# First attention rewritten: q and k stacked in high and low parts, P scaled while it is flipped, V stationary, output projection begun early

## The reference, cut to what matters

```
def _fox_attention(x, w_in, b_f, w_out):          # 16 heads of 64
    proj = x @ w_in
    q, k, v = heads of proj[..., :d], [d:2d], [2d:3d]
    c = cumsum(log_sigmoid(proj[..., 3*d:] + b_f))
    logits = q @ k.T * 64**-0.5 + c[q] - c[k]     # causal: k <= q
    p = softmax(logits)
    return merge(p @ v) @ w_out
```

## Time and profile before

| | us |
|---|---|
| median of 3 runs (2490.05 to 2502.78) | 2502.63 |
| the profiled execution | 2500.41 |
| its span, first to last instruction | 2498.2 |
| busy in the span: TensorE, VectorE, ScalarE, GpSimd | 2328.3, 1084.2, 969.5, 827.3 |
| busy from 0 to 340 us, fp32r projection matmuls with 512 columns, three groups | 161.2 |
| the same, plain fp32 value matmuls PS<-aV,aPT, 320 records | 47.7 |

### The profile page before, as it was taken

The page is one execution under the profiler, slowest core; times in us unless marked ns, Lnnn a source line. Parts: engine busy times, 40 slices in busy tenths (PEclk is TensorE's granted clock), DMA queues, the critical chain, the costliest instruction groups (busy, mean ns, idle before and its releaser), DMA issues.

```text
span 2498.2 us, 28179 instructions
## 1 busy us (share of the span) xinstructions
PE 2328.3 (93%) x11008; PEld 1848.6 (74%) x11008; DVE 1084.2 (43%) x1702; ACT 969.5 (39%) x1929; POOL 827.3 (33%) x616
## 2 busy tenths in 40 slices
PE   8999999999989989899999968997899997999997
PEld 6777678888877766678888857664488886888886
DVE  3333355544344566555553342555555233333322
ACT  4333344443235455354443244443244333333221
POOL 1111064433444333444333442002432335322232
PEclk9999899999989998899999969997899997999998
DMA  4011012222312110122222201010012221222221
GB/s 181 34 51 51 34 63 99 92 101 95 105 53 68 51 51 35 51 73 96 101 99 93 103 11 68 34 34 17 1 43 77 101 101 51 102 97 89 97 98 58
DMA packets 26773, 178.88 MB, mean 72 GB/s; under 512 B 2961, under 2 KB 3089, under 8 KB 8849
## 3 DMA queue, kind: packets, MB, share of 16 engines
q1 hardware_dynamic: 26640, 177.08, 20.2%
HBM read 174.97 MB, written 2.10 MB: 71 GB/s over the span
## 4 chain that ended last, share of the span: by engine, by line
PE 88%; DVE 4%; ACT 4%; POOL 2%; issue 2%; DMA 0%; POOLq 0%; ACTq 0%; SPq 0%; DVEq 0%
PE PS L1150 85%; PE PS L1239 1%; POOL XL L2186 1%; PE PS L1330 1%; DVE cCVT L2070 0%; PE PS L1276 0%; POOL A_p L2206 0%; ACT bP L1576 0%; POOL A_c L2206 0%; ACT HI L1418 0%; POOL A_a L2208 0%; DVE bST L1940 0%; DVE YH L1806 0%; PE PS L1256 0%; POOL A_a L2206 0%
## 5 line engine op out<-in xcount | busy, mean ns | idle before, releaser
L2186 POOL TENSOR_TENSOR LO<-RAW,HI 128x512 fp32r<-128x512 f32 (+1 forms) x334 | 483.0, 1463 | 946.4 <-ACT HI L1418 946.4
L1150 PE MATMUL PS<-XH,HI 128*128 128x512 f32 (+1 forms) x1584 | 651.7, 411 | 37.9 <-POOL XL L2186 20.5
L1150 PE MATMUL PS<-XL,HI 128*128 128x512 f32 (+1 forms) x1584 | 625.9, 395 | 0.0
L1150 PE MATMUL PS<-XH,LO 128*128 128x512 f32 (+1 forms) x1584 | 625.9, 395 | 0.0
L1735 DVE TENSOR_TENSOR LO<-RAW,HI 128x512 fp32r<-128x512 f32 (+1 forms) x334 | 359.2, 1080 | 332.4 <-ACT HI L1418 332.1
L1418 ACT ACTIVATE HI<-RAW 128x512 fp32r<-128x512 f32 (+3 forms) x668 | 365.4, 607 | 178.5 <-PE PS L1150 171.7
L1150 PEld LDWEIGHTS PS<-XH,HI 128*128 128x128 f32 (+1 forms) x1584 | 303.1, 191 | 124.4 <-issue 56.0
L1150 PEld LDWEIGHTS PS<-XH,LO 128*128 128x128 f32 (+1 forms) x1584 | 301.5, 190 | 66.1 <-issue 1.4
L1150 PEld LDWEIGHTS PS<-XL,HI 128*128 128x128 f32 (+1 forms) x1584 | 303.1, 191 | 53.5 <-issue 1.1
L1150 PE MATMUL PS<-HH,HI 128*128 128x512 f32 x528 | 205.4, 389 | 0.0
L1150 PE MATMUL PS<-HL,HI 128*128 128x512 f32 x528 | 205.4, 389 | 0.0
(11 more groups left out here) (368 smaller groups left out, 3193.7 us busy)
## 6 DMA issues: line engine op xcount, KB each, us to landing
RAW<-wall SPq DMA_DIRECT2D x138, 1024.0 KB, 4.8
RAW<-wall SPq DMA_DIRECT2D x24, 896.0 KB, 4.6
RAW<-wall SPq DMA_DIRECT2D x5, 512.0 KB, 3.5
XF<-xT SPq DMA_DIRECT2D x4, 512.0 KB, 5.5
outT<-XR SPq DMA_DIRECT2D x8, 256.0 KB, 2.0
FP<-cfp SPq DMA_DIRECT2D x1, 1024.0 KB, 6.8
MKF<-cmask SPq DMA_DIRECT2D x1, 704.0 KB, 11.1
RAW<-wall SPq DMA_DIRECT2D x1, 640.0 KB, 3.9
```

The lines of the kernel that those rows point to most:

```text
L1150: return e.matmul(out, a, b, start=start, stop=stop)
L2186: return e.tensor_tensor(out, x, h.bitcast(F32), ALU.subtract)
```

## The change

- **q and k.** A q tile is evacuated (`qeq`) into four half-height copies by ScalarE (each head's high part on both halves of the 128 rows) and two low parts by VectorE; a k tile (`qek`) into two high parts by ScalarE and two low parts on the other half by VectorE. The other half beside q's low part is filled with zeros once (`zero`). A score block is then two fp32r matmuls over 128 rows and the mask. Everything is double buffered by head pair.
- **P.** The logits and the exponentials share one of three buffers aP. A new step `dg` (VectorE) makes the reciprocal of the row sum and multiplies the identity with it; the flip is a plain fp32 matmul of the P block with this diagonal. A new step `ft` cuts the flipped block into a high part (ScalarE) and a low part (VectorE).
- **Values.** The four steps of a head are now its key blocks. V's high or low part (two heads side by side, 128 columns) is stationary, P moves with 512 to 128 columns, three fp32r matmuls each. The result is feature-major already, and its half is cut into aOH and aOL by ScalarE and VectorE; the turn is gone. v is kept in two buffers of four heads in high and low parts (`avs`).
- **Order.** Stages scores, dg, flip, ft, values with lags 0, 1, 2, 3, 7; the first v unit comes before the attention starts; the units are q1 q2 v1 q3 q4 v2 q5 q6 v3 q7; the rate is 1.05. The first output projection unit is put with its two tiles side by side while the attention goes on at 2.2 steps per tick, each contraction tile after its pair of heads.
- **Memory.** aNB, aDG and aNC lie where the rotation tables go; the tables' load moves behind the unit ("up0", 4).

```diff
 
 
+LAGF = (0, 1, 2, 3, 7)
 LAGS = (0, 2, 3, 5)
 LAGD = (0, 1, 2, 3, 4)
-RATES = (1.0, 0.85, 1.15, 0.36, 1.0)
+RATES = (1.05, 0.85, 1.15, 0.36, 1.0)
...
         def qkunit(hp):
-            t0, t1 = lin_fm(("aqk", hp), "X")
-            s = put("qev", hp, t0, t1)
-            freed[tiles[t0].bank], freed[tiles[t1].bank] = ("qev", s), ("kev", s)
+            def evac(j, t):
+                freed[tiles[t].bank] = ("kl", put("qek", hp, t)) if j else ("ql", put("qeq", hp, t))
+            lin_fm(("aqk", hp), "X", evac=evac)
+            units["q"] = hp + 1
 
...
 
+        def diag(it):
+            put("dg", *it)
+            yield from ()
+
         def flip(it):
-            h, i = it
-            b, s = turn_bank(), ("fl", h, i)
+            at_bank(put("fl", *it), turn_bank())
+            yield
+
+        def taken(it):
+            freed[ag.bank_of[("fl",) + it]] = ("ptl", put("ft", *it))
+            yield from ()
+
+        def values(it):
+            h, kb = it
+            while units["v"] <= h // 4:
+                yield
+            b, s = 6 + h % 2, ("va", h, kb)
             at_bank(s, b)
             put(*s)
-            freed[b] = ("pta" if i % 2 else "ptd", s)
+            if kb == 3:
+                freed[b] = ("ol", s)
+                done[0] = h + 1
+                if h % 2:
+                    ready["aO", h // 2] = ("ol", s)
             yield
 
...
+        put("zero")
         qkunit(0)
-        units["q"] = 1
         lin["banks"] = [0, 1]
+        lin["n"] = 1
         chores.append(gates(t))
         put("cst")
-        alongside(staggered([(h, i) for h in range(16) for i in range(4)], [scores, flip, values, turn], LAGS), RATES[0])
-        for kind, i in [("v", 0), ("q", 1), ("v", 1), ("q", 2), ("q", 3), ("v", 2), ("q", 4), ("q", 5), ("v", 3),
-                        ("q", 6), ("q", 7)]:
+        vunit(0)
+        alongside(staggered([(h, i) for h in range(16) for i in range(4)], [scores, diag, flip, taken, values], LAGF), RATES[0])
+        for kind, i in [("q", 1), ("q", 2), ("v", 1), ("q", 3), ("q", 4), ("v", 2), ("q", 5), ("q", 6), ("v", 3), ("q", 7)]:
             if kind == "q":
                 if i >= 2:
-                    until(lambda: done[0] >= 2 * i - 2)
+                    until(lambda: sent[0] >= 8 * i - 8)
                 qkunit(i)
             else:
+                if i >= 2:
+                    until(lambda: done[0] >= 4 * i - 4)
                 vunit(i)
-            units[kind] = i + 1
+
+        def reached(kk):
+            if ("aO", kk) not in ready:
+                until(lambda: ("aO", kk) in ready)
+        beside[1] = 2.2
+        ts = lin_fm(("ao", 0), "aO", together=True, before=reached)
         drain()
-        lin["banks"] = [0, 1, 2, 3, 4, 7]
-
-    def attn_out(name, src, n):
+        lin["banks"] = [2, 3, 4, 7, 0, 1]
+        lin["n"] = 0
+        return ts
```

```diff
-            if i == 5:
+            if ag.order[i] == ("up0", 4):
+                e.wait_ge(*when("mx", "sc", 15, 3))
+                e.wait_ge(*when("flip", "fl", 15, 3))
                 e.dma_start(FP[:, 1152:3200], cfp[:, 1152:3200]).then_inc(s_tab, 16)
...
+                kl, o = 128 * (i + 1), PS[bank][:, 0:128 * (i + 1)]
+                q, k = 3072 * (h // 2 % 2) + 512 * (h % 2), 3072 * (h // 2 % 2) + 2048 + 512 * (h % 2)
+                mm(o, aQS[:, q + 128 * i:q + 128 * i + 128], aQS[:, k:k + kl], True, False)
+                mm(o, aQS[:, q + 1024 + 128 * i:q + 1024 + 128 * i + 128], aQS[:, k:k + kl], False, False)
                 mm(PS[bank][:, 128 * i:kl], IDB, CAUS, False, True).then_inc(SEM["qk"], 1)
...
+                n = 4 * h + i
+                e.wait_ge(*when("dg", "dg", h, i))
                 for kb in range(i + 1):
-                    m = e.transpose(PS[bank][:, 128 * kb:128 * kb + 128], p[:, 128 * kb:128 * kb + 128], IDN)
+                    m = mm(PS[bank][:, 128 * kb:128 * kb + 128], aP[:, 512 * (n % 3) + 128 * kb:512 * (n % 3) + 128 * kb + 128], blk(aDG, n % 2, 128))
...
+                h, kb = a
+                if kb == 0:
+                    e.wait_ge(*when("ptl", "ft", h, 3))
+                    if h % 4 == 0:
+                        e.wait_ge(*when("vl", *whole["avs", h // 4, 3]))
+                v = 1024 * (h // 4 % 2) + 256 * kb + 128 * (h // 2 % 2)
+                p = 1664 * (h % 2) + 512 * kb
+                x = slice(p, p + 512 - 128 * kb)
+                o = PS[bank][:, 128 * kb:512]
+                mm(o, aVH[:, v:v + 128], aPH[:, x], kb == 0, False)
+                mm(o, aVH[:, v:v + 128], aPL[:, x], False, False)
+                mm(o, aVL[:, v:v + 128], aPH[:, x], False, kb == 3).then_inc(SEM["pv"], 1)
```

ScalarE's and VectorE's shares of the new steps:

```diff
+            elif kind == "zero":
+                e.wait_ge(*when("xl", "xs", 7))
+                e.wait_ge(s_in, 32)
+                for u in (0, 3072):
+                    act(aQS[64:128, u + 1024:u + 1536], IDN[64:128, 0:1].to_broadcast([64, 512]), ACT.Copy)
+                    m = act(aQS[0:64, u + 1536:u + 2048], IDN[0:64, 64:65].to_broadcast([64, 512]), ACT.Copy)
+                m.then_inc(SEM["zero"], 1)
...
+                if i > 1:
+                    e.wait_ge(*when("pv", "va", 4 * i - 5, 3))
+                v = 1024 * (i % 2) + 256 * c
+                act(aVH[:, v:v + 256], PS[ag.tiles[t].bank][:, 0:256], ACT.Copy).then_inc(SEM["vh"], 1)
...
+                u = 3072 * (hp % 2)
+                ps = PS[ag.tiles[t].bank]
+                for x in range(2):
+                    r = slice(64 * x, 64 * x + 64)
+                    act(aQS[64 - 64 * x:128 - 64 * x, u + 512 * x:u + 512 * x + 512], ps[r, :], ACT.Copy)
+                    m = act(aQS[r, u + 512 * x:u + 512 * x + 512], ps[r, :], ACT.Copy)
+                m.then_inc(SEM["qh"], 1)
+            elif kind == "qek":
+                hp, t = a
+                e.wait_ge(*when_(ag.tiles[t].full))
+                u = 3072 * (hp % 2) + 2048
+                for x in range(2):
+                    r = slice(64 * x, 64 * x + 64)
+                    m = act(aQS[r, u + 512 * x:u + 512 * x + 512], PS[ag.tiles[t].bank][r, :], ACT.Copy)
+                m.then_inc(SEM["kh"], 1)
...
+                p = blk(aP, n % 3)[:, 0:kl]
+                act(p, p, ACT.Exp, bias=aNM[:, n:n + 1], accum_out=aSU[:, n:n + 1]).then_inc(SEM["exp"], 1)
...
+                e.wait_ge(*when("flip", "fl", h, i))
+                if h > 1 and i == 0:
+                    e.wait_ge(*when("pv", "va", h - 2, 3))
+                p = 1664 * (h % 2) + 128 * i
+                act(aPH[:, p:p + 384 * (i + 1)].rearrange("p (k n) -> p k n", n=384)[:, :, 0:128],
+                    PS[ag.bank_of["fl", h, i]][:, 0:128 * (i + 1)].rearrange("p (k n) -> p k n", n=128), ACT.Copy).then_inc(SEM["pth"], 1)
+            elif kind == "va" and a[1] == 3:
+                h, kb = a
+                r = slice(64 * (h % 2), 64 * (h % 2) + 64)
+                e.wait_ge(*when("pv", *step))
+                act(blk(aOH, h // 2)[r, :], PS[bank][r, :], ACT.Copy).then_inc(SEM["oh"], 1)
```

```diff
+            elif kind == "avs":
+                i, c, t = a
+                v = 1024 * (i % 2) + 256 * c
+                e.wait_ge(*when("vh", *step))
+                diff(aVL[:, v:v + 256], PS[ag.tiles[t].bank][:, 0:256], aVH[:, v:v + 256]).then_inc(SEM["vl"], 1)
+            elif kind == "qeq":
+                hp, t = a
+                e.wait_ge(*when("qh", *step))
+                u = 3072 * (hp % 2)
+                for x in range(2):
+                    r, c = slice(64 * x, 64 * x + 64), u + 512 * x
+                    m = diff(aQS[r, c + 1024:c + 1536], PS[ag.tiles[t].bank][r, :], aQS[r, c:c + 512])
+                m.then_inc(SEM["ql"], 1)
+            elif kind == "qek":
+                hp, t = a
+                e.wait_ge(*when("kh", *step))
+                u = 3072 * (hp % 2) + 2048
+                for x in range(2):
+                    r, c = slice(64 * x, 64 * x + 64), u + 512 * x
+                    m = diff(aQS[64 - 64 * x:128 - 64 * x, c:c + 512], PS[ag.tiles[t].bank][r, :], aQS[r, c:c + 512])
+                m.then_inc(SEM["kl"], 1)
...
-                if n > 1:
-                    e.wait_ge(*when("exp", "sc", (n - 2) // 4, (n - 2) % 4))
-                e.tensor_tensor_reduce(blk(aL, n % 2)[:, 0:kl], PS[bank][:, 0:kl], blk(aNB, h % 2)[:, 0:kl], 0.125, -3.0e38,
+                if n > 2:
+                    e.wait_ge(*when("flip", "fl", (n - 3) // 4, (n - 3) % 4))
+                e.tensor_tensor_reduce(blk(aP, n % 3)[:, 0:kl], PS[bank][:, 0:kl], blk(aNB, h % 2)[:, 0:kl], 0.125, -3.0e38,
                                        ALU.add, ALU.max, mx).then_inc(s_vv, 1)
...
+            elif kind == "dg":
                 h, i = a
-                n, kl = 4 * h + i, 128 * (i + 1)
-                e.wait_ge(*when("flip", *step))
+                n = 4 * h + i
+                e.wait_ge(*when("exp", "sc", h, i))
+                e.reciprocal(aRC[:, n:n + 1], aSU[:, n:n + 1]).then_inc(s_vv, 1)
+                vv += 1
```

(15 more changed lines are left out.)

172 lines of the change are left out of this document (67 added, 105 removed).

## The result

The changed kernel takes 2545.48 us (median of 4 runs, 2528.42 to 2547.18), 1.0158 times the time before, with a 95% interval of 1.0093 to 1.0222. The forecast was 2486 with a range of 2464 to 2509, so the change is slower by about 40 us where I had 16 us faster. First the page's head and its chain by engine, which answer to the earlier trace rows.

A forecast was written before the change was run, and what follows sets the result against it. TensorE bounded the kernel before; after, the ScalarE-VectorE loop was to set the weave. Start +1.7, weave -6.5 and tail -11 gave -16 us, 2486 against the median of 2502.63, range 2464 to 2509.

The forecast's parts named there:

- TensorE: First attention, matmul prices per head: scores save 2.03 us, values 0.32, turns 0.22, flips add 1.1; net 1.47 saved.
- the saving of 22 us: TensorE's net saving in the weave (attention steps between projection units), -28.4 - 6.2 + 14.9 - 2.6, allowing 201 us.
- the weave of 217: Attention steps woven between ten projection units, 43.8 to 267.3 us: forecast 217 us, 6.5 less, bounds 201 and 248.
- The rival by which a flip costs four transposes: Flips in the first attention cost 0.44 us each, 35 us on the forecast, 2521 us; chance 3%.
- What then is late, ScalarE and VectorE: In the weave the two engines take turns in one loop: 10.4 us per head plus 4.6 not covered, 15 us.
- k's low part: Weave, where a pair's first scores wait for it at heads 2, 6, 10, 14: 2 us more each, 8 in all.
- the bound for "nothing covered": Slow bound of the weave, no interleaved ScalarE or VectorE work hidden: 14 x 17.7 = 248 us.
- The loop as the bound, the rival at 17.7 us per head: ScalarE-VectorE loop sets the weave: weave +24, start +1.7, tail -5, total 2523 us; chance 13%.
- The waits lower the clock: In the weave TensorE's waits bring the lower clock: 10 us, v chunks 5 more, about 2502 us; chance 17%.
- Start: Start of the weave: v0's extra differences and q's four copies cost 1.7 us, bounds 0 to 4.
- Tail and projection, -11: Attention's rest after the weave plus first output projection unit: 44.1 us before, 33 after; 40 if clock stays low.
- SyncE, the table load: The 1 MB table load, moved behind the fifth unit, delays one unit's load by about 3 us, hidden.

The follow-up runs named there:

- a_nbbank: Changed kernel with the gate row's bank taken from the value banks 6 and 7, out of the flips' rotation: 2519.67 us.
- b_stack: Kernel before the change with only the stacked q and k (fp32r scores over 128 rows): 2495.95 us, ratio 0.9949.
- a_nb_noft: a_nbbank without the 64 differences of the flipped probabilities, values taking the high part in place of the low: 2496.41 us.
- a_spread: a_nbbank with differences of q, k, v and attention output one to three steps behind their copies, q's copies in two portions: 2503.13 us.
- a_spread_swap_r: a_spread with the diagonal ahead of the flipped probabilities' copy and difference, and attention steps per unit matmul at 0.97 instead of 1.05: 2497.19 us.
- a_slack: a_nbbank with flip, split and values one turn later each and a fourth buffer of probabilities: 2525.71 us.

## Why the prediction was wrong

*TensorE.* The prices of the new matmuls were right, the saving of 22 us was not. It does not enter the weave of 217, which the loop set, but it is the gain for which the change was made. Busy less low clock fell from 211.8 to 200.9 us, by 11. Summed from start to start out of the two traces, without pauses and with stretches at the lower clock counted at half, the weave had 212.8 us of TensorE and has 203.5:

```
                    scores, masks  gate rows  flips  values  turns  projections
before                       42.6        2.8   10.5    25.7    2.1        129.0
after                        20.9        5.4   27.4    24.2      -        125.5
```

Scores, masks and values gave 23.2 us and the projection matmuls beside them 3.5, together 26.7 where the text had 34.6. (Why the projections gain: a 64-row fp32 score record started 0.327 us after a 512-column projection matmul, a 128-row fp32r one starts after 0.233, both medians.) The gate row, in no term of the sum, took 2.6 us more, and flips added 16.9 for 14.9, less 2.1 for the turns. About 3 us of the loss go with the pauses, at each of which the last matmul runs its 0.40 us out instead of being followed after 0.23: a_nbbank, with 17 pauses for 33, has 200.8 us by the same sum. b_stack says the same from the other side: 22 us saved where the stacking was priced at 28. The rival by which a flip costs four transposes is out: 0.115 us a record, two records. For this shape a plain fp32 matmul costs twice a transpose (0.23 us against 0.11), where the Trainium skill (TensorE: Matmul & The Clock Gate, Terms) has four times.

*What then is late, ScalarE and VectorE.* **This is the step that failed.** It took 15 us per head and priced k's low part as the only wait of TensorE; the weave took 257.5 us, 18.4 per head, 40 over the forecast and 9 over the bound for "nothing covered". The work was right: 250 us on the two engines against 256 in the text, and k's low part cost 3.4 us in two waits, where the text put 8 on top of what was there. The share not covered rested on a wrong sum besides: the parts listed (1.6, 1.7, 0.7 and 3) add to 6.9 us per head and not to 8.3, and the bound of 17.7 takes 7.3. What I left out was TensorE as a member of the loop. I costed each split as a duration on two engines and asked neither which bank it holds nor what is queued behind it. The runs put numbers to it: the gate row's bank 26 us (of which 22 stand in weave and tail); the bursts of q, k, v and output, during which VectorE idles in front of a block's evacuation, 17 us. With both mended the kernel is at 2503, 17 over the forecast, and its profile has a weave of 226.7 for 217, a tail of 40.5 for 33, and a start of 48.7 for 45.5. That rest has no shown cause.

*The loop as the bound, the rival at 17.7 us per head.* It had the side and not the size (2523), and not the mechanism: the total of the two engines is 97% of the weave, not 118%, and the orders that made the turn less serial cost time. Besides the bank, what helped was spreading the bursts, less work (a_nb_noft) and a slower rate.

*The waits lower the clock.* Right as a mechanism and half of its size: 0.95 over 257.5 us is 12.9 us at the price of half speed, against 4.5 before, 8 more where the rival had 15. It was a rival for itself in the text; here it comes on top of the other waits.

*Start.* 3.0 us for 1.7, inside its bound of 4.

*Tail and projection, -11.* Came out at +1.5. The clock rose from 0.77 to 0.85 as I had hoped, and TensorE was busy 35.2 us, less than 39.8; but it idled 10.7 us, 6.8 of them for aPL in five waits. I take it that the last heads have the same split with less work beside it; no run shows that. In the kernel before, the same part brings nothing; there were only 4.6 us of idle time in its tail.

*SyncE, the table load.* Nothing of it shows.

Open: why a_spread's order, and no other that I tried, suits the turn; what sets its last 20 us of idle time; whether values one turn further behind the split would help, alone or with the late difference; and the rate's own share in a_spread_swap_r.

## What to carry to other kernels

When an evacuation turns from one copy into a copy and a difference on another engine, list every user of its bank and every step queued behind it on both engines before summing durations; a helper that hands out banks in rotation may give one to something unrelated. Read the waits of the engine that is not the bound too: 81 us of VectorE waiting for ScalarE's copies led to the second cause, which TensorE's waits did not name. When a step is moved by a turn, count the distance to each step that reads it or reuses its bank: a_slack moved two together and left the distance that mattered as it was. Before starting work early, read the idle time and the clock of the stage to be filled, not its length: here 4.6 us of 44.4 were idle, and no gain showed. Price what is saved as carefully as what is added, with every record of the step in the sum, the gate row too.

## What the runs showed of the hardware

The granted clock of the weave is lower in the runs in which TensorE idles more, but loosely: 0.98 at 20.3 us idle, 0.95 at 43.8, 0.91 at 94.2, and also 0.91 at 55.9, 0.93 at 31.0 and 0.96 at 31.2. It isn't the sum alone: b_stack has 0.94 at 14.0 us, where the kernel before has 0.98 at 7.0. Of the 22 us that the stacking saved on TensorE, 7 came back there as idle time and 8.5 as low clock.

The same instructions took 8.5 us more in one profiled execution than in another (2195.2 and 2186.7), and the lower clock accounts for the whole: a difference of that size in a stage that the change doesn't touch needs no other reason.

A 64x512 difference takes 0.69 us and a 64x512 copy 0.59, what the 128-row ones take (0.68 and 0.58): a tile of q or k that is taken in two halves by head costs twice the time of one whole.
